# Three quarters of the first feed-forward matrix by seven half-size products per pair of blocks

## What is computed

```python
    h = rms_norm(x, norm_g[l, 2])                       # x: 1024 x 1024
    f = jnp.square(jax.nn.relu(h @ w_ff1[l])) @ w_ff2[l]   # 1024 x 4096, 4096 x 1024
    x = x + rms_norm(f, norm_g[l, 3])
```

## Time and profile before

| | |
|---|---|
| median of 3 runs | 1978.13 us |
| the profiled execution's own time | 1978.7 us |
| its span | 1976.8 us |
| granted TensorE clock, mean | 0.992 |
| PE busy | 1934.8 us, 98% |
| PEld (weight load) busy | 1572.5 us, 80% |
| DVE busy | 941.1 us, 48% |
| ACT busy | 758.9 us, 38% |

### The profile page before, as it was taken

The page is one execution under the profiler, slowest core; times in us unless marked ns, Lnnn a source line. Parts: engine busy times, 40 slices in busy tenths (PEclk is TensorE's granted clock), DMA queues, the critical chain, the costliest instruction groups (busy, mean ns, idle before and its releaser), DMA issues.

```text
span 1976.8 us, 25186 instructions
## 1 busy us (share of the span) xinstructions
PE 1934.8 (98%) x9812; PEld 1572.5 (80%) x9812; DVE 941.1 (48%) x1266; ACT 758.9 (38%) x1163; POOL 82.8 (4%) x63
## 2 busy tenths in 40 slices
PE   8999999998999999999999999999999999999996
PEld 6887777776878888788787888888888888888885
DVE  6715566674435454523446554774333223223446
ACT  6335555554353433533334344543232113202331
POOL 0000000000202122120000000000000000000000
PEclk9999999999999999999999999999999999999998
DMA  5223122213122221222524444432211111111144
GB/s 186 103 100 115 49 97 100 92 60 128 65 96 86 96 86 54 78 83 102 186 100 163 149 142 145 150 133 96 98 52 53 53 42 46 50 53 42 59 144 149
DMA packets 62048, 191.75 MB, mean 97 GB/s; under 512 B 6720, under 2 KB 6784, under 8 KB 61952
## 3 DMA queue, kind: packets, MB, share of 16 engines
q1 hardware_dynamic: 59648, 186.23, 27.1%
q10 hardware_dynamic: 2304, 4.20, 0.6%
HBM read 146.33 MB, written 44.07 MB: 96 GB/s over the span
## 4 chain that ended last, share of the span: by engine, by line
PE 93%; DVE 3%; DMA 2%; ACT 1%; issue 1%; SPq 0%; DVEq 0%; ACTq 0%
PE gemm L339 18%; PE gemm L341 17%; PE gemm L340 17%; PE gemm L582 5%; PE gemm L584 5%; PE gemm L583 5%; PE dn L1319 2%; PE dn L1317 2%; PE z L1216 2%; PE gemm L1404 2%; PE dn L1238 2%; PE gemm L1406 2%; PE gemm L1405 2%; PE dn L1280 1%; PE dn L1315 1%; PE attn_out L1250 1%
## 5 line engine op out<-in xcount | busy, mean ns | idle before, releaser
L339 PE MATMUL gemm<-act_hi,w_hi 128*128 128x512 f32 x1216 | 501.8, 413 | 0.8 <-issue 0.5
L341 PE MATMUL gemm<-act_hi,w_lo 128*128 128x512 f32 x1216 | 476.0, 391 | 0.0
L340 PE MATMUL gemm<-act_lo,w_hi 128*128 128x512 f32 x1216 | 475.1, 391 | 0.0
L331 DVE TENSOR_TENSOR w_lo<-w_raw,w_hi 128x1024 fp32r<-128x1024 f32 x174 | 213.3, 1226 | 189.3 <-ACT w_hi L326 185.8
L326 ACT ACTIVATE w_hi<-w_raw 128x1024 fp32r<-128x1024 f32 x174 | 183.1, 1052 | 285.8 <-PE gemm L341 153.2
L341 PEld LDWEIGHTS gemm<-act_hi,w_lo 128*128 128x128 f32 x1216 | 228.8, 188 | 49.5
L339 PEld LDWEIGHTS gemm<-act_hi,w_hi 128*128 128x128 f32 x1216 | 229.8, 189 | 47.0 <-issue 7.2
L340 PEld LDWEIGHTS gemm<-act_lo,w_hi 128*128 128x128 f32 x1216 | 230.0, 189 | 43.2 <-issue 3.8
L385 ACT ACTIVATE stage<-gemm,cols 128x512 f32<-128x512 f32 x104 | 71.6, 689 | 213.9 <-PE gemm L341 209.4
L1088 ACT ACTIVATE f_t<-f_t 128x512 f32<-128x512 f32 x64 | 40.4, 632 | 218.0 <-DVE f_t L1916 218.0
L1586 DVE TENSOR_TENSOR_SCAN a_P<-a_keep,a_P,a_floor 128x512 f32<-128x512 f32 (+3 forms) x96 | 94.0, 1007 | 37.6 <-ACT a_keep L883 37.3
(11 more groups left out here) (272 smaller groups left out, 2880.2 us busy)
## 6 DMA issues: line engine op xcount, KB each, us to landing
w_raw<-w_stream SPq DMA_DIRECT2D x174, 512.0 KB, 3.4
projections<-stage SPq DMA_DIRECT2D x60, 512.0 KB, 2.9
gate<-projections SPq DMA_DIRECT2D x48, 256.0 KB, 2.8
d_in<-projections SPq DMA_DIRECT2D x12, 512.0 KB, 7.1
x_sb<-xT SPq DMA_DIRECT2D x8, 512.0 KB, 9.2
x_fin<-xT SPq DMA_DIRECT2D x8, 512.0 KB, 4.3
residual<-mixed ACTq DMA_DIRECT2D x16, 256.0 KB, 2.0
act_hi<-residual SPq DMA_DIRECT2D x8, 512.0 KB, 4.9
```

The costliest lines, as they stand in the source:

```text
L331: nc.vector.tensor_tensor(lo[s][:], raw[s][:].rearrange("p (k c) -> p k c", k=KT), hi[s][:].bitcast(f32), ALU.subtract).then_inc(lo_ready[ ...
L339: nc.tensor.matmul(g_bank[hf][:], w_hi[s][:, k, :], a_hi[:, k, t], start=(k == 0), stop=False)
L340: nc.tensor.matmul(g_bank[hf][:], w_hi[s][:, k, :], a_lo[:, k, t], start=False, stop=False)
L341: last = nc.tensor.matmul(g_bank[hf][:], w_lo[s][:, k, :], a_hi[:, k, t], start=False, stop=(k == KT - 1))
```

## The change

The first matrix of groups 1 to 3 is no longer computed block by block. Twelve steps `m` (pairs of blocks 52 to 63) each take two blocks of weights. A pair of output tiles, the two halves of the input features (tiles 0 to 3 and 4 to 7) and the two halves of the positions make a product of 2x2 by 2x2 quarters, and that is computed with seven products of quarters and not eight (Winograd's form of Strassen's scheme). A quarter product is four 128x128 tiles by 512 positions, three matmuls each: 12 matmuls. For it there are

- four sums of quarters of the activation (`sums_x1`, in `mixed`, once), with their upper and lower parts in `q_hi`, `q_lo` and, for product 6, in place in `act_hi`, `act_lo`;
- four sums of quarters of the weights per pair (`weights_sum`, DVE, in `s_t`), with their upper parts (`later_upper`, ACT) and lower parts (`later_lower`, DVE) in `s_hi`, `s_lo` and the first half of `w_hi[1]`;
- three copies of running totals out of PSUM per pair (`copy_product`, ACT), three additions and four roots (`hidden`, DVE).

The order on TensorE is 1, 2, 6, 5, 7 of pair 0, and then for each pair: product 1 of the next one, 4 and 3 of this one, 2, 6, 5, 7 of the next one. All this is written out without loops.

The hidden values of all groups (`f_t` after the square, float32) are stored to DRAM (`fT`, 256 KB each) and loaded again: those of group 0 in eight loads of 512 KB into `mixed` near the end of the products, the others in 256 KB pieces into `f_stage` one or two blocks ahead. Their upper and lower parts are made then (`hidden_upper`, `hidden_lower`), in turn into `act_hi`/`act_lo` and `f_hi`/`f_lo`. So all of the first matrix now comes before all of the second. Group 0 of the first matrix still runs in two half passes, now one straight after the other; the eight x1 tiles of the second half stand all beside the first pass, and in ACT's order ahead of the block's square; the scaling and sums of x1 stand beside the second. The second matrix's groups 0 to 2 take both halves of a block, its last group runs in half passes as before. Four pair loads of weights fall away (88 turns become 84).

```diff
-PAIR_FULL = 60
-PAIR_LAST = 80
-N_TURNS = 88
+PAIR_ST = 52
+N_ST = 12
+PAIR_F2 = 64
+PAIR_LAST = 76
+N_TURNS = 84
 N_PAIRS = 72
...
-        TILES_FF1 = [[], [], [0], [], [1], [], [2], []]
-        TILES_FF2 = [[3], [4], [5], [6], [7], [], [], []]
+        TILES_FF1 = [[], [0], [1], [2], [3], [4], [5, 6], [7]]
...
+        SEQ = [(0, p) for p in (1, 2, 6, 5, 7)]
+        for m in range(N_ST):
+            SEQ += ([(m + 1, 1)] if m + 1 < N_ST else []) + [(m, 4), (m, 3)]
+            SEQ += [(m + 1, p) for p in (2, 6, 5, 7)] if m + 1 < N_ST else []
...
+            def store_hidden(e, row, hf):
+                sp.wait_ge(f_sqr, e + 1)
+                sp.dma_start(fT[row, :, half_of(hf)], f_t[e % 2][:]).then_inc(f_st[e % 2], 16)
+            for hf in range(2):
+                for b, n, s in half_pass(PAIR_FF + 4 * hf):
+                    store_hidden(8 * hf + b, b, hf)
+                    load_weights(sp, n + 2, s, back=4 if n + 2 < PAIR_FF + 4 else 8 if n + 2 < PAIR_ST else 4) if n + 2 <= PAIR_ST else None
...
+                if i and (m, p) == (N_ST - 2, 3):
+                    for v in range(2):
+                        sp.wait_ge(f_st[v], FST0[v] + 16 * 8)
+                    sp.wait_ge(t_lo, TLO0 + 16)
+                    for k in range(KT):
+                        sp.dma_start(mixed[:, k, :], fT[k]).then_inc(f_ld[k % 2], 16)
...
+            def square_hidden(e):
+                act.wait_ge(*((bank_read[e % 2], 1 + FILLS_OUT + PAIR_FF - PAIR_OUT + e // 2 + 1) if e < 16 else (st_f, F0 + e - 16 + 1)))
+                nc.scalar.activation(f_t[e % 2][:], f_t[e % 2][:], ACT.Square).then_inc(f_sqr, 1)
...
+            def later_upper(m, p):
+                act.wait_ge(st_sum, SUM0 + 4 * m + {5: 1, 7: 2, 6: 3, 3: 4}[p])
+                if m:
+                    act.wait_ge(st_mm, MM[m - 1, p])
+                elif p == 5:
+                    act.wait_ge(blk_done[1], PAIR_ST)
+                hi, lo, k = W_OF[p]
+                nc.scalar.activation(hi[:, k:k + 4, :], s_t[{5: 0, 7: 1, 6: 2, 3: 0}[p]][:, 0:HALF].rearrange("p (k c) -> p k c", c=P), ACT.Copy).then_inc(st_hi, 1)
...
+            def copy_product(m, p):
+                act.wait_ge(st_mm, MM[m, p])
+                if m:
+                    act.wait_ge(st_add, ADD0 + 3 * (m - 1) + ADDS[{1: "11", 6: "12", 7: "22"}[p]])
+                nc.scalar.activation({1: p_first, 6: p_second, 7: p_third}[p], z_bank[m % 2][:], ACT.Copy).then_inc(st_copy, 1)
...
             for hf in range(2):
-                for b, n, s in half_pass(PAIR_FF + 8 * hf):
+                for b, n, s in half_pass(PAIR_FF + 4 * hf):
                     if b == 0:
                         inverse_norm(act, hf, root_x1, c_total, c_ln, c_root)
                         if hf == 0:
                             inverse_norm(act, 1, root_out, o_total, o_ln, o_root)
-                    ff_upper(b, hf, s, 8 * hf + b, 1 + FILLS_OUT + n - PAIR_OUT + 1)
-                    split_hi(act, n + 1, s)
                     if hf == 0:
                         for k in TILES_FF1[b]:
                             take_x1(1, k)
-                for b, n, s in half_pass(PAIR_FF + 8 * hf + 4):
+                    square_hidden(8 * hf + b)
+                    if n + 1 < PAIR_ST:
+                        split_hi(act, n + 1, s)
+                    if hf:
+                        if b == 0:
+                            act.wait_ge(c_lo, 2 * KT)
+                            for v in range(2):
+                                act.wait_ge(x1_st[v], 16 * KT)
+                        if b < 4:
+                            scaled_x1(b)
+                            scaled_x1(4 + b)
+                        if 2 <= b < 6:
+                            for p in (5, 7, 4):
+                                sum_upper(b - 2, p)
+                        if b == 5:
+                            later_upper(0, 6)
+                        if b == 6:
+                            first_upper(0)
...
+                if i and m == N_ST - 1 and p in (6, 5, 7, 4):
+                    if p == 6:
+                        split_hi(act, PAIR_F2, 0)
+                    for j in range(2):
...
+            def seventh(m, p):
+                n = PAIR_ST + m
+                if p in LATER:
+                    pe.wait_ge(st_lo, LO0 + 4 * m + LATER[p])
+                else:
+                    pe.wait_ge(lo_ready[0 if p < 4 else 1], n + 1)
+                if m == 0 and p in (6, 5, 7, 4):
+                    pe.wait_ge(t_lo, TLO0 + (16 if p == 6 else 12))
+                if p == 1 and m >= 2:
+                    pe.wait_ge(st_f, F0 + 4 * (m - 2) + EVENTS["21"])
+                if p == 2 and m:
+                    pe.wait_ge(st_add, ADD0 + 3 * (m - 1) + ADDS["11"])
+                if p == 5 and m:
+                    pe.wait_ge(st_add, ADD0 + 3 * (m - 1) + ADDS["12"])
+                if p in (6, 7, 4):
+                    pe.wait_ge(st_copy, COPY0 + 3 * m + COPIES[{6: 1, 7: 6, 4: 7}[p]])
+                if p == 3:
+                    pe.wait_ge(st_add, ADD0 + 3 * m + ADDS["22"])
+                hi, lo, k0 = W_OF[p]
+                o = product_bank(m, p)[:]
+                for k in range(4):
+                    one = nc.tensor.matmul(o, hi[:, k0 + k, :], quarter(p, 0)[:, k, :], start=(k == 0 and p in (1, 2, 5)), stop=False, skip_group_check=True)
+                    if k == 0 and p in (6, 3):
+                        one.then_inc(blk_done[0 if p == 6 else 1], 1)
+                    nc.tensor.matmul(o, hi[:, k0 + k, :], quarter(p, 1)[:, k, :], start=False, stop=False, skip_group_check=True)
+                    last = nc.tensor.matmul(o, lo[:, k0 + k, :], quarter(p, 0)[:, k, :], start=False, stop=(k == 3), skip_group_check=True)
+                last.then_inc(st_mm, 1)
...
+            def ff_root(e, hf):
+                if e >= 2:
+                    dve.wait_ge(f_st[e % 2], FST0[e % 2] + 16 * (e // 2))
+                nc.vector.scalar_tensor_tensor(f_t[e % 2][:], g_bank[e % 2][:], 0.0, root_x1[:, half_of(hf)], ALU.max, ALU.mult).then_inc(bank_read[e % 2], 1)
+            def sums_x1(kk):
+                dve.wait_ge(t_scl, TSCL0 + 2 * kk + 2)
+                a, c = mixed[:, kk, half_of(0)], mixed[:, kk, half_of(1)]
+                d, e = mixed[:, 4 + kk, half_of(0)], mixed[:, 4 + kk, half_of(1)]
+                nc.vector.tensor_tensor(a, c, a, ALU.subtract).then_inc(t_sum, 1)
+                nc.vector.tensor_tensor(c, e, c, ALU.subtract).then_inc(t_sum, 1)
+                dve.wait_ge(t_sum, TSUM0 + 4 * kk + 1)
+                nc.vector.tensor_tensor(e, e, a, ALU.subtract).then_inc(t_sum, 1)
+                dve.wait_ge(t_sum, TSUM0 + 4 * kk + 3)
+                nc.vector.tensor_tensor(d, d, e, ALU.subtract).then_inc(t_sum, 1)
...
+            def weights_sum(m, p):
+                one, two = w_raw[0], w_raw[1]
+                if p == 5:
+                    if m:
+                        dve.wait_ge(st_lo, LO0 + 4 * m)
+                    for s in range(2):
+                        dve.wait_ge(raw_loaded[s], 16 * (PAIR_ST + m) + 16)
+                    nc.vector.tensor_tensor(s_t[0][:], two[:, 0:HALF], two[:, HALF:2 * HALF], ALU.add).then_inc(st_sum, 1)
+                elif p == 7:
+                    nc.vector.tensor_tensor(s_t[1][:], one[:, 0:HALF], two[:, 0:HALF], ALU.subtract).then_inc(st_sum, 1)
+                elif p == 6:
+                    dve.wait_ge(st_sum, SUM0 + 4 * m + 1)
+                    nc.vector.tensor_tensor(s_t[2][:, 0:HALF], s_t[0][:], one[:, 0:HALF], ALU.subtract).then_inc(st_sum, 1)
+                else:
+                    dve.wait_ge(st_lo, LO0 + 4 * m + LATER[5])
+                    dve.wait_ge(st_sum, SUM0 + 4 * m + 3)
+                    nc.vector.tensor_tensor(s_t[0][:], one[:, HALF:2 * HALF], s_t[2][:, 0:HALF], ALU.subtract).then_inc(st_sum, 1)
...
+            def hidden(m, c):
+                e = event(m, c)
+                f = f_t[e % 2][:]
+                dve.wait_ge(f_st[e % 2], FST0[e % 2] + 16 * (e // 2))
+                if c == "21":
+                    dve.wait_ge(st_mm, MM[m, 4])
+                    whole = z_bank[m % 2][:]
+                else:
+                    kept, bank_of, done, copied = {"11": (p_first, c_bank, 2, 1), "22": (p_third, o_bank, 5, 7), "12": (p_second, o_bank, 3, 6)}[c]
+                    dve.wait_ge(st_mm, MM[m, done])
+                    dve.wait_ge(st_copy, COPY0 + 3 * m + COPIES[copied])
+                    nc.vector.tensor_tensor(f, kept, bank_of[:], ALU.add).then_inc(st_add, 1)
+                    dve.wait_ge(st_add, ADD0 + 3 * m + ADDS[c])
+                    whole = f
+                nc.vector.scalar_tensor_tensor(f, whole, 0.0, root_x1[:, half_of(int(c[1]) - 1)], ALU.max, ALU.mult).then_inc(st_f, 1)
...
+                for b, n, s in half_pass(PAIR_FF + 4 * hf):
                     if hf == 0:
                         x1_tiles(1, TILES_FF1[b])
+                    else:
```

(28 more changed lines are left out.)

322 lines of the change are left out of this document (232 added, 90 removed).

## The result

The changed kernel takes 1982.51 us (median of 14 runs, 1977.67 to 1985.15) where the kernel before takes 1978.26 us on the same chips (14 runs). The ratio is 1.0022, interval 1.0014 to 1.003: 4.3 us slower. The prediction was 1977.5 us and "no change". The time lies in its range; the call does not hold, since the slowdown is larger than what the measurement leaves open. The question is which terms of a sum of losses, 32.0 us by the prediction, came out about 5 us too small.

What follows compares the result with a forecast made beforehand. Feed-forward stage bound by the number of matmuls, 226 ns each. Terms -32.6 + 21.2 + 0 + 5.3 + 5.5 = -0.6 us; median 1978.1 - 0.6 = 1977.5 us, no change that counts; range 1967 to 1988.

Steps and rivals of the forecast that it cites:

- The saving of 32.6 us: First matrix, twelve pairs: 84 matmuls each instead of 96, so 144 fewer at 0.2261 us, -32.6 us.
- The steady state: Seven products per pair: DVE and ACT keep ahead, tightest chain 6.9 us against 8.0, cost 0, bounds 0 and +12.
- The first pass's cycle of 6.5 us: Group 0, first pass: DVE and ACT take 6.5 us a block against TensorE's 5.44; 8.9 us lost in the pass.
- the second's of 7.0 and 8.8: Group 0, second pass, with x1 sums: 7.0 us a block for blocks 1 and 2, 8.8 for 3 and 4.
- The walk to the first product: Both passes of group 0, block by block: first product at 1368.3 instead of 1346.4, +21.2 us after today's waits.
- half clock before block 8: Group 0: 3.7 us idle before block 8 lowers TensorE's clock, delaying its total and all that follows by about 1.5 us.
- Rival 2: First group: the queues keep ahead, 1953 us; if only the second pass does, 1965; chance 0.12 with that half.
- rival 1: TensorE keeps its clock: the idle stretches of 3.7 to 5.3 us cost only themselves, 1972 us; chance 0.16.
- rival 3: Seven products wait in every pair, product 4 behind ACT's copy of product 7: slower, 1986 to 1992 us; chance 0.20.
- The clock: Half clock after idle stretches: 1.5 us before block 8, 2.0 each before first product and last product 4; +5.5 us.
- The end of the products: Last product 4 waits for ACT's copy behind group 0's loads, landing 14.5 us after request: +5.3 us, bounds 1.1 and 11.
- Second matrix and last pass: After the products: about 4 us of DVE and 2 of ACT per 10.9 us block, last pass as before; cost 0.

Runs made afterwards that it cites:

- experiment 8: Experiment 4 plus three small edits: pair 1's weight sums later, one quarter split later, first two hidden loads ahead of half a weight load; 1946.97 us, ratio 0.984.
- experiment 5: Changed kernel, loads still late, but in the last pair hidden tiles 0 to 5 are taken only behind the copy of product 7; 1979.01 us, ratio 1.0005.
- experiment 1: Changed kernel, first pass reordered: x1 tile behind the block's square and upper split (ACT) and behind its root (DVE), one per block; 1973.25 us, ratio 0.9977.
- experiment 2: Changed kernel, second pass reordered: DVE's root before x1 sums and spread-out quarter splits, weight sums behind the first lower split; 1966.93 us, ratio 0.9955.
- experiment 7: Kernel before, full-size products, with x1 tiles moved into blocks 1 to 7 of the first pass, ahead of root and square; 1992.6 us, ratio 1.0064.
- experiment 6: Changed kernel plus unused constant products while TensorE would wait, before the first product and the last product 4; 1975.61 us, ratio 0.9989.
- experiment 3: Changed kernel with the eight loads of group 0's hidden values issued during pair 1 of the products instead of pair 10; 1972.61 us, ratio 0.9973.
- experiment 4: Changed kernel with the edits of experiment 1, experiment 2 and experiment 3 together; 1953.36 us, ratio 0.9878.

## Why the prediction was wrong

**What held.** The saving of 32.6 us, less 1.6 of waits (experiment 8). The steady state at no cost: between the first product and the last product 4 nothing waits. The first pass's cycle of 6.5 us (6.53 to 6.55), and the second's of 7.0 and 8.8 (6.96 and 8.76 between roots). The walk to the first product: forecast 1368.3 without the clock's part, which is 104.8 us behind the group's first matmul at 1263.48. Experiment 5's trace has the same code up to there and no half clock before block 8, and has 104.9. Experiments 1, 2 and 7 show that these losses come from the order, as the walk said. Rival 2, the queues keep ahead, fell with them; rival 1 fell with the four stretches at 0.50 and with experiment 6, though other executions lack some of these stretches; rival 3 did not happen in the changed kernel.

**What failed** is the sizes of three terms of the sum, the clock, the end of the products and the second matrix, all in one direction. The changed kernel's trace:

| term | forecast | measured | too small by |
|---|---|---|---|
| first group, without the clock (from experiment 5's trace) | 21.2 | 21.3 | 0.1 |
| half clock before block 8 (the rest of 24.1) | 1.5 | 2.8 | 1.3 |
| wait before the last product 4 | 5.3 | 7.3 | 2.0 |
| second matrix's start | 0 | 1.3 | 1.3 |
| half clock after first product and last product 4 | 4.0 | 4.8 | 0.8 |

The 24.1 is the first product's start against TensorE's own pace from the start of the group (24.8), less the 0.7 us that the prediction takes for the waits of before. (Only 0.3 us of that 0.7 lies in this stretch, by the profile's list of waits: the earlier trace rows counts from 1100 us. It is the same 0.7 in both columns.) Together 5.5 us: -0.6 becomes +4.9. The last matmul of the kernel starts 3.6 us later than before (1965.24 against 1961.62), the median is 4.3 up. Of the 1.3 us between 4.9 and 3.6, 0.5 is the group's own earlier start in this execution (1263.00 against 1263.48), and 0.5 is that the kernel's last two matmuls start 0.54 us apart and not 1.01 as before, in a part that nobody changed. The other 0.3 stays open.

**First mis-sized term, "The clock".** The half clock before block 8 was priced at 1.5 us and cost 2.8, and the two on the chain behind it cost 4.8 and not 4.0. The step that failed is the price of the first, which delays everything behind it: its 12 spacings at 0.43 us carry straight through the total of the squares into the second pass, whose first root comes at 1319.62, where experiment 5's trace without the half clock has it at 1316.88. How many matmuls run slowly there is not the same each time: in the five traces with this same first pass it is 12 (the changed kernel), 8, 8, 0 and 0 (experiments 3, 6, 2, 5). The forecast's 1.5 would have been about right for two of them.

**Second mis-sized term, "The end of the products": 5.3 forecast, 7.3 measured.** By the forecast's numbers the last product 4 was due 14.5 + 2.1 + 0.6 - 5.3 = 11.9 us after the request for group 0's loads. In the trace it was due 11.0 us after it, 1603.70 less the 7.3, against 1585.32: the request stood 0.9 us later in the order of the products than I had it. That is one half. The other is the landing: 14.5 us after the request by forecast, and 15.6 by ACT's start at 1600.88. The transfers between 1585 and 1601 us came to:

```profile
DMA packets 1713, 5.48 MB, mean 342 GB/s; under 512 B 193, under 2 KB 193, under 8 KB 1713
```

The rate is not where the forecast was off. Its own 4.95 MB in 14.5 us are 341 GB/s as a mean over the whole batch, and 342 came (351 from the request to the last landing). (4.95 MB at 397 GB/s take 12.5 us and not the 12.7 that the prediction writes; its 14.5 is the 12.5 and the 2 around it.) What was more is the traffic, 5.48 MB: three stores of 256 KB fall into these 16 us where I counted one. But that is not the whole of it either, for the same batch with the same stores was faster in most other traces:

| trace | request | last of the eight landed | us |
|---|---|---|---|
| changed kernel | 1585.32 | 1600.81 | 15.5 |
| experiment 1 | 1577.50 | 1592.44 | 14.9 |
| experiment 2 | 1571.30 | 1585.32 | 14.0 |
| experiment 3 (early) | 1412.83 | 1426.96 | 14.1 |
| experiment 4 (early) | 1394.63 | 1408.88 | 14.3 |
| experiment 5 | 1581.61 | 1595.81 | 14.2 |
| experiment 6 | 1580.95 | 1595.03 | 14.1 |
| experiment 8 (early) | 1387.46 | 1401.44 | 14.0 |

So 14.5 was a fair size, the changed kernel's profiled execution landed late, and why is open; its eight landings come 1.3 us apart but for the seventh, which took 2.2. Experiment 2, with the landing at 14.0, still waited 5.9 us before that product (from start to start, beyond the pace), so the late request alone keeps the wait above the 5.3. The Trainium skill, "DMA: Bandwidth & Descriptors", Where 436 GB/s comes from, gives 358 GB/s for such loads. By it, as an estimate, the 4.95 MB would take 13.8 us and land at 15.8, 1.3 us later than forecast (the prediction says 1.1). That is near this one trace, but above all eight, and 390 GB/s were moved here from 1590 to 1600 us. The trace does not bear the page out as a limit.

**The missed term** is "Second matrix and last pass ... Cost 0"; 1.3 us were measured. I had costed the work (4 us of DVE in 10.9) and not the chain: the lower split of the weights starts at 1612.93, SP's loads of the first hidden tiles stand behind the weight loads that wait for that split, and they land 5.6 us after ACT is free for them:

```profile
1614.16 0.93 SPq L338 DMA_DIRECT2D w_raw<-w_stream  x2
1615.20 7.94 SPq L889 DMA_DIRECT2D sum_x<-hidden  x3
...
1621.43 1.28 ACT L1261 ACTIVATE f_hi<-sum_x 128x512 fp32r<-128x512 f32 x2 [5.58 <-DMA sum_x<-hidden]
```

Experiment 5 made that chain longer and the wait grew to 3.2 us; experiment 8 took the hidden loads out from behind the weight load and it is gone (experiments 3 and 4, in which no late load delays the last products, still had 0.7 and 1.2 us of it, so the chain alone makes the greater part).

A sum of -32.6 and +32.0 says little of its sign: an error of a sixth in the losses was enough. The chance of "slower" that I gave rested almost wholly on rival 3 and not on the walk's own small terms, of which the second matrix's 0 could only come out larger. That the time came out within 5 us is in part luck, since the clock before block 8 alone is worth 0 to 2.8 us from one execution to the next.

## What to carry to other kernels

When a change saves matmuls on a kernel bound by TensorE and adds side work to engines that are half idle, the saving comes whole only if each queue's order lets it: walk one block through both queues, and put first what TensorE waits for next (here root, square and the weights' upper split), and side work, above all work that waits for a load, behind it. The same instructions in three other places were worth 29 us here, where the change had cost 4.3. A batch of loads should be asked for as early as its buffer is free; "just in time" cost 10 us.

## What the runs showed of the hardware

A gap of 3.4 to 7.6 us between two matmul starts was followed each time in the changed kernel by 10 to 14 matmul starts 0.43 us apart at a granted clock of 0.50, 2.2 to 3.0 us lost each time. It is not the same in every execution. Behind the same wait before block 8 (3.8 us from start to start), the traces of experiments 2 and 5 show the clock at 1.00; experiment 5's window, to be read against the changed kernel's 12 matmuls in 5.00 us:

```profile
1308.79:1314.00 5.21, 5.21 (x23) 4.32 (x24) 4.44 (x7) 1.28 (x3) 0.00 (x0) 1.00 0.44 151
```

So a difference of up to 3 us between two single executions can be this clock alone. The 14 runs of the changed kernel spread over 7.5 us and the ten each of experiments 1, 3, 5 and 6 over 4.9 to 9.0; the four of experiment 8, with no long idle stretch in this part, over 2.9, but four say little, for those of experiment 4 spread over 0.8. Products that serve nothing, issued while TensorE would wait, kept the clock at 1.00 in both places and gave back 4.8 us there by the trace.

The part ahead of the feed-forward stage, which no edit touches, ends between 1261.9 and 1265.2 us in these traces. Where two traces are compared to a microsecond, it is best done from the group's first matmul: so counted, the changed kernel is 4.1 us slower than before, experiment 7 is 14.4 slower, experiments 4 and 8 are 24.3 and 31.0 faster, each within 0.3 of its medians. Experiments 1 and 5, whose runs spread wide, lie 1.7 and 1.8 us off theirs (6.2 and 0.7 faster by the trace, 4.5 faster and 1.1 slower by the medians).
